# A two-layer decoder trunk: mask set-up, the last block of layer 0, the last gate tile and the last row re-staged

## Chip, cores and metric

The kernel runs on one core of one Trainium2 chip. The metric is the device time of the program in microseconds, the median of three runs. A profiled execution of the same program gives the trace.

## The reference

Input x is 1024 tokens by 1024 channels in float32. Each of two layers adds a mixer of the RMS-normed input to it, and a final RMS norm follows.

```python
# layer 0: gated linear attention (4 heads) beside RWKV-7 (8 heads), chunks of 64 tokens
h = h + (concat(gla, rwkv) * silu(gate)) @ w_out0
# layer 1: q, k, v, gate = rmsnorm(h) @ w_in1 + b; 128-token window, sinks, 16 heads
p = exp(s - m); denom = sum(p) + exp(sink - m)
h = h + ((p / denom) @ v * silu(gate)) @ w_out1 + b_out1
return rmsnorm(h, final_norm_w)
```

RWKV-7 updates a state S = S diag(w) + (S a) b + v k for every token; the kernel solves blocks of it as triangular systems.

## The kernel before, in words

Engines work in program order and meet through semaphores. Three blocks follow each other; all engines leave a block together and enter the next. SyncE (SP) issues all DMAs, in the order in which they are written down.

`project0` norms and turns x, then runs 30 tiles of 128 output columns of layer 0's input projection. Each weight tile arrives by a load, GpSimd (POOL) splits it into a high and a low part (`split_parts`, L1484 and L1488), TensorE (PE) forms three products for each of two halves of 512 tokens (`products3`, L1496), and ScalarE (ACT) keeps the result. VectorE (DVE) works on it; its last operations follow the GLA tiles, n = 14 to 17. The tiles n = 22 to 29 are the gate. At n = 17, 23 and 27 SP spills keys, the GLA's queries and keys (`QK`, the upper half of `VQ`) and values.

`chunks0` is the recurrence, eight blocks of 128 tokens (`ND` = 8), software-pipelined over steps p. Before the steps, SP loads `maska`, `inner`, `maskb`, `maskd` (L702 to L704) and then the first spilled blocks. DVE folds the masks into `near` and `first`, scales `bdones` into `RB`, builds `eye` (L1289 to L1294); ACT fills six buffers from `eye` (L1443, L1444); POOL clears buffers (`zeroed`). PE does `cross(0)` (L848), DVE keeps it under the mask `inner` (`keep_cross`, L1158) and `keep_first_turned` (L1165, L1172), then PE does `near_and_gla(0)` (L860, L865), DVE `keep_products(0)` (L1179, L1182), PE the first join (L877). `RB` is read by `bonus_sums` (L1033). Two steps behind, `output_products` (L1047) multiplies a block by the output weights in two halves of 512 columns; `add_output` (L1276) adds the residual, `square_row` (L1425 to L1430), `invert_row` (L1283) and `norm_row` (L1438) norm the row in place once its un-normed form has been stored to `h1_dram` (L736).

`layer1_stage` turns the normed rows (`turn_rows`, L1708) in 16 groups of four transposes over four banks; ACT keeps the high part of each (L1847), DVE the low part (`low`, L1906). `project_values` (L1496, columns of 256) starts after the tenth group and needs `WVH` and `WVL`, split by POOL (L1484, L1488). Eight value products and 18 tiles follow (8 query, 2 key, 8 gate). In the last tile (n = 17), `scores(0)` and `scores(1)` stand between the halves. Attention is 64 steps g, eight query pairs for each of eight blocks: PE does `scores(g)` (L1735) and `turn_probs(g - 2)` (L1746), DVE `mask_and_max(g)` (L1920) and every other copy of turned probabilities (L1992), ACT two exponentials (L1879) and the other copies (L1873). Every four steps the denominators are inverted (L1934, L1936), turned by PE (`turn_sums`, L1753, first at g = 7), kept (L1941), sent through `es_dram` and spread over the partitions (`spread_sums`), POOL multiplies the gate by them (`scale_gate`, L1679) and DVE gates the values' products (L1946, from g = 13). POOL also stages the next block (`stage`) and splits the output weights (`weights`).

At the end PE forms the output products row by row (L1773, `done`), DVE adds two halves (L2003), ACT squares and roots the row (L1889, L1891), DVE inverts and scales it (`finish`, L1951, L1953), one row behind except for the last, and SP stores it (L1623).

## Time and profile before

| | |
|---|---|
| Median of three runs | 1205.45 us (1202.07 to 1209.12) |
| The profiled execution | 1204.18 us |
| Its span, first to last instruction | 1202.4 us |
| Mean granted TensorE clock | 0.973 |
| PE, DVE, ACT, POOL busy | 1131.1, 532.8, 364.5, 405.7 us |

A row's start is in microseconds from the span's start. The layer 0 tiles end at about 378, the recurrence at about 748, the tiles of layer 1 at about 985, attention at about 1098. A granted clock of 1.00 stands for TensorE's 2.4 GHz, 0.50 for 1.2 GHz. Names of buffers can be those of a buffer that shares the memory.

### The profile page before, as it was taken

The numbers are of one execution on the slowest core, as the hardware profiler recorded it, in microseconds if no ns is written. First come the engines' busy times: TensorE is split into PE (matmuls) and PEld (weight loads), VectorE is DVE, ScalarE is ACT, GpSimd is POOL, SyncE is SP. The second block draws the span as 40 slices with busy tenths as digits, with TensorE's granted clock in tenths as the row PEclk, the third lists the DMA queues.
The fourth block names the chain that finished last, engine by engine and source line by source line (L and its number), as shares of the span: only waits on it lengthen the run. The fifth ranks groups of instructions, "written<-read, shape, count | busy, mean of one in ns | idle before, by whom it ended". The sixth has DMA issues, their size and how long they took to land. (4 is left out here: it accounts for less than half of the span.)

```text
span 1202.4 us, 26513 instructions
## 1 busy us (share of the span) xinstructions
PE 1131.1 (94%) x11544; PEld 855.9 (71%) x11544; DVE 532.8 (44%) x953; ACT 364.5 (30%) x835; POOL 405.7 (34%) x284
## 2 busy tenths in 40 slices
PE   5999999999996899999999997899999989999897
PEld 4777778788885777667666653888888875556785
DVE  5588886510001344344444321525550018995333
ACT  6343432520111233133323322300111027774111
POOL 2223232433331112122212221412333456773752
PEclk9999999999998788999999999899999999999999
DMA  6111102614302311022111113201111112223311
GB/s 252 35 36 52 35 18 71 192 53 122 122 35 96 130 56 43 26 63 73 29 55 46 39 37 104 85 18 53 52 36 51 52 36 62 72 63 92 137 53 70
DMA packets 60024, 82.83 MB, mean 69 GB/s; under 512 B 3200, under 2 KB 45200, under 8 KB 59536
## 3 DMA queue, kind: packets, MB, share of 16 engines
q1 hardware_dynamic: 59920, 81.30, 21.2%
q8 instruction: 82, 1.34, 0.5%
q14 instruction: 22, 0.18, 0.1%
HBM read 64.45 MB, written 16.84 MB: 68 GB/s over the span
## 5 line engine op out<-in xcount | busy, mean ns | idle before, releaser
L1496 PE MATMUL ps<-HNH,WH 128*128 128x512 f32 x736 | 289.9, 394 | 0.0
L1496 PE MATMUL ps<-HNL,WH 128*128 128x512 f32 x736 | 286.4, 389 | 0.0
L1496 PE MATMUL ps<-HNH,WL 128*128 128x512 f32 x736 | 286.4, 389 | 0.0
L1496 PEld LDWEIGHTS ps<-HNH,WH 128*128 128x128 f32 x736 | 138.2, 188 | 31.0 <-issue 2.7
L1496 PEld LDWEIGHTS ps<-HNH,WL 128*128 128x128 f32 x736 | 138.2, 188 | 30.4 <-issue 1.9
L1496 PEld LDWEIGHTS ps<-HNL,WH 128*128 128x128 f32 x736 | 138.2, 188 | 28.9
L1920 DVE CUSTOM_DVE_ANT_0 AR<-ps,GV,nsink 128x256 f32<-128x256 f32 x128 | 56.4, 478 | 89.8 <-PE ps L1735 89.7
L1047 PE MATMUL ps<-VQ,BK 128*128 128x512 f32 x128 | 66.6, 624 | 4.1 <-POOL BK L799 2.2
L1879 ACT ACTIVATE AR<-AR,nm 128x256 f32<-128x256 f32 x128 | 63.6, 499 | 16.6 <-DVE nm L1920 16.6
L1484 POOL CAST WH<-WA 128x1024 fp32r<-128x1024 f32 x16 | 19.1, 1195 | 136.6 <-PE ps L1496 106.9
L1047 PE MATMUL ps<-WO,BK 128*128 128x512 f32 x128 | 64.9, 619 | 0.0
L1484 POOL CAST WH<-GV 128x1024 fp32r<-128x1024 f32 x18 | 18.7, 1041 | 135.7 <-PE ps L1496 135.7
L1285 DVE MEMSET small<- 128x1 f32 x1 | 0.1, 59 | 129.6 <-PEq L232 129.6
L1773 PE MATMUL ps<-HNH,WH 128*128 128x512 f32 x128 | 51.1, 399 | 3.0 <-POOL WL L1647 3.0
L1773 PE MATMUL ps<-HNH,WL 128*128 128x512 f32 x128 | 50.6, 395 | 0.0
L1773 PE MATMUL ps<-HNL,WH 128*128 128x512 f32 x128 | 50.4, 393 | 0.0
L1746 PE MATMUL ps<-ident,AR 128*128 128x128 f32 x256 | 44.2, 298 | 3.1 <-ACT AR L1879 3.1
L877 PEld LDWEIGHTS ps<-shared,GV 64*64 64x64 f32 x1024 | 37.5, 148 | 11.4 <-issue 10.3
L1488 POOL TENSOR_TENSOR WL<-GV,WH 128x1024 fp32r<-128x1024 f32 x18 | 43.2, 2400 | 2.6 <-POOL WH L1484 2.2
L1187 DVE COPY_PREDICATED shared<-near,ps 128x256 f32<-128x256 int32 x32 | 13.8, 433 | 64.5 <-PE ps L877 64.5
L877 PE MATMUL ps<-shared,GV 64*64 64x32 f32 x1024 | 40.1, 230 | 1.5 <-DVE GA L1182 0.9
L1488 POOL TENSOR_TENSOR WL<-WA,WH 128x1024 fp32r<-128x1024 f32 x16 | 39.4, 2460 | 2.1 <-POOL WH L1484 1.4
(288 smaller groups left out, 2000.3 us busy)
## 6 DMA issues: line engine op xcount, KB each, us to landing
GV<-in_w1t SPq DMA_DIRECT2D x18, 512.0 KB, 3.5
AR<-in_x SPq DMA_DIRECT2D x16, 512.0 KB, 5.4
WA<-in_w0t SPq DMA_DIRECT2D x16, 512.0 KB, 3.5
RAW<-in_w0t SPq DMA_DIRECT2D x8, 512.0 KB, 3.8
bk_dram<-BK SPq DMA_DIRECT2D x1, 4096.0 KB, 17.2
RAW<-bk_dram SPq DMA_DIRECT2D x8, 512.0 KB, 5.7
h_dram<-AR SPq DMA_DIRECT2D x8, 512.0 KB, 3.4
GV<-es_dram SPq DMA_DIRECT2D x32, 128.0 KB, 3.0
```

The source lines that it names most:

```text
L877: last = pe.matmul(bank[4][half(e), h * B:(h + 1) * B], BA[d % 2][half(e), a, q, 0, :], x[half(e), h, :], start=True, stop=True)
L1047: last = pe.matmul(bank[5][:], SG[:, k, tokens(d)], WO[k // PAIRS][:, k % PAIRS, h * HB:(h + 1) * HB], start=(k == 0), stop=(k == KT - 1))
L1187: dve.copy_predicated(TM[l][:], near[:, l].unsqueeze(1).to_broadcast([P, HEADS, B]), bank[4][:, 0:HEADS * B].rearrange("p (h t) -> p h t", ...
L1285: dve.memset(leps, LN_EPS)
L1484: eng.tensor_copy(high, raw).then_inc(parts, 1)
L1488: eng.tensor_tensor(low, raw, high.bitcast(F), ALU.subtract).then_inc(parts, 1)
L1496: last = pe.matmul(out, a, b, start=(k == 0 and i == 0), stop=(k == n - 1 and i == 2))
L1746: last = pe.transpose(PS[4 + t % 2][:, (2 * a + b) * P:(2 * a + b + 1) * P], PR[:, t % 3, a, b * P:(b + 1) * P], ident[:])
L1773: last = pe.matmul(PS[2 * (t % 4) + h][:], a[:, (t + 1) % 2, k, :], w[:, k, cols], start=(k == 0 and m == 0), stop=(k == KT - 1 and m == 2 ...
L1879: ins = act.activation(PR[:, g % 3, a, :], PR[:, g % 3, a, :], ACT.Exp, scale=-1.0, bias=nm[:, h:h + 1], accum_out=rs[:, h:h + 1])
L1920: ins = dve.tensor_tensor_reduce(PR[:, g % 3, a, :], PS[2 * (j % 2) + a][:, 0:2 * P], band[:, 0 if n == 0 else 1, :], -1.0, nsink[:, h:h + 1],
```

## The change

Masks. `inner`, `near` (now five levels, as many as are read), `first` and `eye` are allocated for all of layer 0. SP loads three masks in `project0` behind tile 25's weights, into the spilled memory of `QK`; DVE folds them behind its last GLA operations. In `chunks0` only `maska` is loaded; DVE starts with `keep_cross`, and `RB` follows `keep_products(0)`. ACT fills `XT0` first.

```diff
                 if n == 23:
                     sp.wait_ge(g_scaled, 4)
                     spill(1, QK.rearrange("p a q t -> p (a q) t"))
+                if n == 25:
+                    sp.wait_ge(spilled[1], 16)
+                    sp.dma_start(inner[:], maska_d).then_inc(masks_in, 16)
+                    sp.dma_start(maskb, maskb_d[:, 0]).then_inc(masks_in, 16)
+                    sp.dma_start(maskd, maskd_d).then_inc(masks_in, 16)
...
                 dve.tensor_tensor(qk, qk, e, ALU.mult).then_inc(g_scaled, 1)
+            dve.wait_ge(masks_in, 48)
+            for e in range(2):
+                dve.memset(inner[e * C:e * C + B, 0, B:C], 0.0)
+            dve.tensor_tensor(near[:], maskd[:, 0:LEVELS - 1, 0:B], maskd[:, 0:LEVELS - 1, B:C], ALU.bitwise_or)
+            dve.tensor_tensor(first[:], maskb[:, 0, :], maskb[:, 1, :], ALU.bitwise_or)
+            dve.tensor_tensor(eye[:], istack[:, 0:B], istack[:, B:C], ALU.add).then_inc(masks_set, 1)
...
     maska = buf("maska", [P, 2, C])
-    near = buf("near", [P, LEVELS, B], I32)
-    first = buf("first", [P, C], I32)
-    inner = buf("inner", [P, 2, C])
+    inner, near, first, eye = presets
...
-            for mask in (maska, inner):
-                sp.dma_start(mask[:], maska_d).then_inc(s["masks_in"], 16)
-            sp.dma_start(maskb, maskb_d[:, 0]).then_inc(s["masks_in"], 16)
-            sp.dma_start(maskd, maskd_d).then_inc(s["masks_in"], 16)
+            sp.dma_start(maska[:], maska_d).then_inc(s["masks_in"], 16)
...
-                after(pe, "masks_set", 1)
+                after(pe, "masks_set", 2)
...
             dve.memset(leps, LN_EPS)
             dve.memset(geps, EPS)
+            keep_cross(BA, 0, inner, "b_prod", "ba_kept")
+            dve.wait_ge(s["presets"], 1)
+            keep_first_turned(0)
             dve.wait_ge(s["masks_in"], 64)
-            for e in range(2):
-                dve.memset(inner[QTR[2 * e][2], 0, B:C], 0.0)
-            dve.tensor_tensor(near[:], maskd[:, :, 0:B], maskd[:, :, B:C], ALU.bitwise_or)
-            dve.tensor_tensor(first[:], maskb[:, 0, :], maskb[:, 1, :], ALU.bitwise_or)
+            dve.wait_ge(s["zeroed"], 1)
+            keep_products(0)
             for q in range(PAIRS):
-                dve.tensor_scalar(RB[:, q, :], bdones[:], col("r_k", q), None, ALU.mult)
-            dve.tensor_tensor(eye, istack[:, 0:B], istack[:, B:C], ALU.add).then_inc(s["masks_set"], 1)
-            dve.wait_ge(s["masks_set"], 1)
-            dve.wait_ge(s["presets"], 1)
-            dve.wait_ge(s["zeroed"], 1)
-            keep_cross(BA, 0, inner, "b_prod", "ba_kept")
-            keep_first_turned(0)
-            keep_products(0)
+                ins = dve.tensor_scalar(RB[:, q, :], bdones[:], col("r_k", q), None, ALU.mult)
+            ins.then_inc(s["masks_set"], 1)
...
-            act.wait_ge(s["masks_set"], 1)
-            for b in TM:
-                act.activation(b[:], eye.unsqueeze(1).to_broadcast([P, HEADS, B]), ACT.Copy)
-            act.activation(XT0[:], eye.unsqueeze(1).to_broadcast([P, HEADS, B]), ACT.Copy).then_inc(s["presets"], 1)
+            for b in (XT0, *TM):
+                ins = act.activation(b[:], eye[:].unsqueeze(1).to_broadcast([P, HEADS, B]), ACT.Copy)
+            ins.then_inc(s["presets"], 1)
```

The last block. The second half of the last output product is added, squared and normed in layer 1's block. POOL writes the normed row to a part of `VQ`, between the two halves of the `WV` split, and the transposes read it there; the store, too, is issued in the new block. The value products start two groups later. ACT waits for the stores before it overwrites the rows.

```diff
             def add_output(d, h):
-                if not 0 <= d < ND:
+                if not 0 <= d < ND or (d, h) == (ND - 1, 1):
                     return
...
-                if not 0 <= d < ND:
+                if not 0 <= d < ND - 1:
...
             def square_row(d):
                 if not 0 <= d < ND:
                     return
+                if d == ND - 1:
+                    after(act, "out_added", 2 * d + 1)
+                    act.wait_ge(s["gated"], d + 1)
+                    act.activation(VT[:, :, tokens(d)], H1[:, 0:PAIRS, tokens(d)], ACT.Square, accum_out=ms[:, d:d + 1]
+                                   ).then_inc(s["half"], 1)
+                    act.wait_ge(s["half"], 3 * d + 1)
+                    act.activation(mb[:, d:d + 1], ms[:, d:d + 1], ACT.Identity, bias=eps, scale=1.0 / D).then_inc(s["half"], 1)
+                    return
...
+            sp.wait_ge(s["out_added"], 2 * TT)
+            sp.dma_start(h1_dram[:, TT - 1, :].rearrange("p (k c) -> p k c", c=P), AR[:, :, last_block]
+                         ).then_inc(h1_out[(TT - 1) % 2], 16)
+            for dst, src in ((BV, bv1), (COS, cos_d), (SIN, sin_d)):
+                sp.dma_start(dst, src).then_inc(s["rope_in"], 16)
             for there in h1_out:
                 sp.wait_ge(there, 16 * TT // 2)
-            for dst, src in ((BV, bv1), (COS, cos_d), (SIN, sin_d)):
-                sp.dma_start(dst, src).then_inc(s["rope_in"], 16)
...
             pool.wait_ge(wv_in, 16)
-            split_parts(pool, WV, WVH, WVL, 2 * W0_TILES, parts)
+            pool.tensor_copy(WVH, WV).then_inc(parts, 1)
+            pool.wait_ge(s["inverted"], 2 * TT)
+            pool.tensor_scalar(last_row, AR[:, :, last_block], last_rs, None, ALU.mult).then_inc(s["normed"], 1)
+            pool.wait_ge(parts, 2 * W0_TILES + 1)
+            pool.tensor_tensor(WVL, WV, WVH.bitcast(F), ALU.subtract).then_inc(parts, 1)
...
+                if g == KT:
+                    pe.wait_ge(s["normed"], TT)
                 for j in range(4):
-                    last = pe.transpose(PS[g % 4][:, j * P:(j + 1) * P], AR[:, k, block_tokens(4 * half + j)], ident[:])
+                    t = 4 * half + j
+                    last = pe.transpose(PS[g % 4][:, j * P:(j + 1) * P], last_row[:, k, :] if t == TT - 1 else
+                                        AR[:, k, block_tokens(t)], ident[:])
...
             for g in range(KT):
                 turn_rows(g)
             for g in range(KT, 2 * KT):
                 turn_rows(g)
-                if g % 2:
-                    project_values((g - KT) // 2)
-            for t in range(TT // 2, TT):
+                if g % 2 and g > KT + 1:
+                    project_values((g - KT) // 2 - 1)
+            for t in range(TT // 2 - 1, TT):
                 project_values(t)
...
+            act.wait_ge(s["out_added"], 2 * TT)
+            act.activation(VQ[:, 0:KT // 2, last_block], AR[:, KT // 2:, last_block], ACT.Square, accum_out=last_ms
+                           ).then_inc(s["half"], 1)
+            act.wait_ge(s["half"], 3 * TT)
+            act.activation(last_ms, last_ms, ACT.Sqrt, bias=last_mb, scale=1.0 / D).then_inc(s["rooted"], 1)
...
+            for there in h1_out:
+                act.wait_ge(there, 16 * TT // 2)
...
+            added = AR[:, KT // 2:, last_block]
+            dve.tensor_tensor(added, added, PS[5][:].rearrange("p (k t) -> p k t", k=KT // 2), ALU.add
+                              ).then_inc(s["out_added"], 1)
             dve.memset(KTT[:, :, 0:P], 0.0)
             dve.memset(V1[:, 0, :], 0.0)
+            dve.wait_ge(s["rooted"], 2 * TT)
+            dve.reciprocal(last_rs, last_ms).then_inc(s["inverted"], 1)
+            for g in range(KT):
+                low(g)
             dve.tensor_scalar(bqs, col("b_q", 0, 8), GLA_SCALE, None, ALU.mult).then_inc(s["bq"], 1)
             dve.tensor_scalar(nsink[:], col("sinks", 0, 16), -1.0, None, ALU.mult).then_inc(s["bq"], 1)
             dve.wait_ge(s["bq"], 2)
-            for g in range(KT):
-                low(g)
             dve.wait_ge(s["rope_in"], 48)
             for g in range(KT, 2 * KT):
                 low(g)
-                if g % 2:
-                    keep_values((g - KT) // 2)
-            for t in range(TT // 2, TT):
+                if g % 2 and g > KT + 1:
+                    keep_values((g - KT) // 2 - 1)
+            for t in range(TT // 2 - 1, TT):
```

The last gate tile. Its first half has SiLU while PE works on the second. Its second half is kept as exp(-x) and as x, POOL adds 1, DVE inverts it in step 4, and POOL multiplies by x between the first two splits of output weights.

```diff
                 sp.wait_ge(s["sums_out"], 16 * (half + 1))
                 if half:
                     sp.wait_ge(s["scaled"], half)
+                else:
+                    sp.wait_ge(s["chain"], 4 * (Q_TILES + 2) + 3)
...
-            pool.wait_ge(s["tile_done"], W1_TILES)
+            pool.wait_ge(s["tile_kept"], W1_TILES + 2)
+            gate = SG1[:, KT - 1, HB:]
+            pool.tensor_scalar(gate, gate, 1.0, None, ALU.add).then_inc(s["chain"], 1)
             def scale_gate(half):
                 pool.wait_ge(s["sums_in"], 32 * (half + 1))
+                if half == HALVES // 2 + 1:
+                    pool.wait_ge(s["chain"], 4 * (Q_TILES + 2) + 3)
                 pool.tensor_tensor(place(half), place(half), RD, ALU.mult).then_inc(s["scaled"], 1)
 
             weights(0)
+            pool.wait_ge(s["chain"], 4 * (Q_TILES + 2) + 2)
+            pool.tensor_tensor(gate, LAST, gate, ALU.mult).then_inc(s["chain"], 1)
...
-                tile_half(n % 2, 0)
+                first = tile_half(n % 2, 0)
                 if n == W1_TILES - 1:
+                    first.then_inc(s["tile_done"], 1)
                     scores(0)
                     scores(1)
                 tile_half(n % 2, 1).then_inc(s["tile_done"], 1)
...
                 if g == 2:
-                    pe.wait_ge(s["tile_kept"], W1_TILES)
+                    pe.wait_ge(s["tile_kept"], W1_TILES - 1)
+                if g == 6:
+                    pe.wait_ge(s["tile_kept"], W1_TILES + 2)
                 if g - 2 < STEPS:
...
-            for j in range(KT):
+            for j in range(KT - 1):
                 keep(W1_GATE + j, SG1[:, j, :], ACT.Silu)
+            act.wait_ge(s["tile_done"], W1_TILES)
+            act.activation(SG1[:, KT - 1, 0:HB], PS[6][:], ACT.Silu).then_inc(s["tile_kept"], 1)
 
             for g in range(STEPS + 2):
                 t = g - 2
+                if t == 0:
+                    act.wait_ge(s["tile_done"], W1_TILES + 1)
+                    act.activation(SG1[:, KT - 1, HB:], PS[7][:], ACT.Exp, scale=-1.0).then_inc(s["tile_kept"], 1)
+                    act.activation(LAST, PS[7][:], ACT.Copy).then_inc(s["tile_kept"], 1)
...
+                if g == 4:
+                    dve.wait_ge(s["chain"], 4 * (Q_TILES + 2) + 1)
+                    dve.reciprocal(SG1[:, KT - 1, HB:], SG1[:, KT - 1, HB:]).then_inc(s["chain"], 1)
```

The last row. PE signals each half; each half is added and squared by itself. POOL multiplies the first half by the final norm's weights; at the end ACT scales the first half while DVE scales the second.

```diff
-                sp.wait_ge(s["normed"], TT + t + 1)
+                sp.wait_ge(s["normed"], TT + t + (2 if t == TT - 1 else 1))
...
+            pool.wait_ge(s["squared"], 2 * TT)
+            pool.tensor_tensor(R[:, TT - 1, 0:HB], R[:, TT - 1, 0:HB], FN[:, 0:HB], ALU.mult).then_inc(s["biased"], 1)
...
-                if i == 2 * KT - 1:
+                if i == 2 * KT - 1 or (t, i) == (TT - 1, KT - 1):
                     last.then_inc(s["done"], 1)
...
+            t = TT - 1
+            act.wait_ge(s["added"], TT)
+            act.activation(SW[:, 0:HB], R[:, t, 0:HB], ACT.Square, accum_out=ms[:, t:t + 1]).then_inc(s["squared"], 1)
+            act.wait_ge(s["squared"], 2 * TT)
+            act.activation(first_half, ms[:, t:t + 1], ACT.Identity, bias=eps, scale=1.0 / D).then_inc(s["squared"], 1)
+            act.wait_ge(s["added"], TT + 1)
+            act.wait_ge(s["squared"], 2 * TT + 1)
+            act.activation(SW[:, HB:T], R[:, t, HB:T], ACT.Square, accum_out=ms[:, t:t + 1]).then_inc(s["squared"], 1)
+            act.wait_ge(s["squared"], 2 * TT + 2)
+            act.activation(sd[:, t:t + 1], ms[:, t:t + 1], ACT.Sqrt, bias=first_half, scale=1.0 / D).then_inc(s["rooted"], 1)
+            act.wait_ge(s["biased"], TT + 1)
+            act.wait_ge(s["inverted"], 3 * TT)
+            act.activation(R[:, t, 0:HB], R[:, t, 0:HB], ACT.Copy, scale=sd[:, t:t + 1]).then_inc(s["normed"], 1)
...
+                cols = slice(HB if t == TT - 1 else 0, T)
+                dve.scalar_tensor_tensor(out=R[:, t, cols], in0=R[:, t, cols], scalar=sd[:, t:t + 1], in1=FN[:, cols],
                                          op0=ALU.mult, op1=ALU.mult).then_inc(s["normed"], 1)
...
                 for h in range(2):
                     cols = slice(h * HB, (h + 1) * HB)
+                    if t == TT - 1 and h:
+                        finish(t - 1)
+                        dve.wait_ge(s["done"], TT + 1)
                     ins = dve.tensor_tensor(R[:, t, cols], R[:, t, cols], PS[2 * (t % 4) + h][:], ALU.add)
-                ins.then_inc(s["added"], 1)
-                if t:
+                    if t == TT - 1 or h:
+                        ins.then_inc(s["added"], 1)
+                if 0 < t < TT - 1:
                     finish(t - 1)
             finish(TT - 1)
```

## Rows read from the trace of the kernel before

**Rows 1.** The page's first part: busy us (share of the span) and instructions of each engine.

```profile
PE 1131.1 (94%) x11544; PEld 855.9 (71%) x11544; DVE 532.8 (44%) x953; ACT 364.5 (30%) x835; POOL 405.7 (34%) x284
```

**Rows 2.** TensorE's waits: line, releaser, us in total, times, longest.

```profile
PE ps L860 <- DVE shared L1165: 10.6, 1, 10.6
...
PE ps L1708 <- PEq L698: 5.5, 1, 5.5
...
PE ps L1746 <- ACT AR L1879: 3.1, 1, 3.1
PE ps L1773 <- POOL WL L1647: 3.0, 1, 3.0
```

**Rows 3.** Timeline of VectorE at the start of the recurrence: start, us, operation, idle before.

```profile
379.81 0.06 DVE L1285 MEMSET small<- 128x1 f32 x1 [129.64 <-PEq L232]
...
388.64 1.23 DVE L1158 TENSOR_TENSOR GV<-ps,inner 128x1024 f32<-128x1024 f32 x1 [2.07 <-issue]
```

**Rows 4.** Timeline of TensorE at the start of the recurrence.

```profile
379.78 1.10 PE L848 MATMUL ps<-AR,RAW 64*64 64x128 f32 x32 [1.43 <-PEq L232]
391.50 0.88 PE L860 MATMUL ps<-RAW,AR 64*32 64x32 f32 x64 [10.62 <-DVE shared L1165]
```

**Rows 5.** Timeline of ScalarE at the start of the recurrence.

```profile
386.61 1.64 ACT L1443 ACTIVATE shared<-OB 128x256 f32<-128x256 f32 x5 [7.13 <-DVE OB L1294]
```

**Rows 6.** Timeline of SyncE at the start of the recurrence.

```profile
381.83 0.36 SPq L710 DMA_DIRECT2D QKS<-qk_dram  x1
```

**Rows 7.** DMA issues: size and median us to landing.

```profile
out<-AR SPq DMA_DIRECT2D x8, 512.0 KB, 2.6
...
QKS<-qk_dram SPq DMA_DIRECT2D x8, 256.0 KB, 3.1
```

**Rows 8.** Timeline of all engines at the entry of layer 1.

```profile
748.87 0.63 ACT L1425 ACTIVATE VQ<-AR 128x512 f32<-128x512 f32 x1 [11.46 <-DVE AR L1276]
...
752.14 1.15 ACT L1438 ACTIVATE AR<-AR,small 128x1024 f32<-128x1024 f32 x1 [1.14 <-DMA h_dram<-AR]
...
753.60 6.76 PE L1708 MATMUL ps<-ident,AR 128*128 128x128 f32 x36 [5.48 <-PEq L698]
...
755.54 4.55 POOL L1488 TENSOR_TENSOR KHL<-GV,Q 128x2048 fp32r<-128x2048 f32 x1
...
755.60 7.50 DVE L1906 SCALAR_TENSOR_TENSOR HNL<-ps,par,HNH 128x512 fp32r<-128x512 f32 x10
...
761.92 0.36 PE L1496 MATMUL ps<-Q,HNH 128*128 128x256 f32 x1 [0.75 <-DVE HNL L1906]
```

**Rows 9.** Groups of instructions on GpSimd by form: busy us, mean ns.

```profile
L1652 POOL TENSOR_TENSOR AR<-AR,KTT 128x1024 f32<-128x1024 f32 x8 | 24.0, 3006 | 0.0
```

**Rows 10.** Timeline of ScalarE behind the last gate tile.

```profile
984.84 1.08 ACT L1853 ACTIVATE VQ<-ps 128x512 f32<-128x512 f32 x2 [10.96 <-PE ps L1496]
985.95 1.28 ACT L1879 ACT_TABLE_LOAD   x1
```

**Rows 11.** Groups of instructions on VectorE by form.

```profile
L1920 DVE CUSTOM_DVE_ANT_0 AR<-ps,GV,nsink 128x256 f32<-128x256 f32 x128 | 56.4, 478 | 89.8 <-PE ps L1735 89.7
L573 DVE RECIPROCAL GV<-GV 128x1024 f32<-128x1024 f32 x4 | 26.2, 6552 | 0.1
```

**Rows 12.** Chain of waits around the first turned denominators.

```profile
997.51 0.21 PE ps L1753
```

**Rows 13.** Busy time by stretch: PE, PEld, DVE, ACT, POOL, granted clock, DMA.

```profile
988.00:998.00 10.00, 9.52 (x48) 6.91 (x49) 6.01 (x22) 7.20 (x28) 3.68 (x3) 0.50 0.36 106
...
1116.00:1121.00 5.00, 5.00 (x15) 3.94 (x16) 1.28 (x2) 1.46 (x3) 5.00 (x3) 0.66 1.00 404
```

**Rows 14.** Timeline of VectorE and SyncE behind the last matmul.

```profile
1194.09 1.28 DVE L2003 TENSOR_TENSOR AR<-AR,ps 128x512 f32<-128x512 f32 x2 [8.20 <-PE ps L1773]
...
1196.79 1.97 SPq L1623 DMA_DIRECT2D out<-AR  x2
...
1197.11 1.28 DVE L1953 SCALAR_TENSOR_TENSOR AR<-AR,small,V 128x1024 f32<-128x1024 f32 x1
```

More of the change, by code:

```diff
@@ L103, in trunk @@
         rms = {n: sem("rms_" + n) for n in ("squared", "rooted", "inverted")}
-        rows = {n: sem("rows_" + n) for n in ("done", "added", "normed")}
+        rows = {n: sem("rows_" + n) for n in ("done", "added", "normed", "out_added", "half")}
         def row_turn():
@@ L145, in trunk @@
             bk_in0 = sem("bk_in0")
+            inner = sb("inner", [P, 2, C], ctx=layer0)
+            near = sb("near", [P, LEVELS - 1, C // 2], I32, ctx=layer0)
+            eye = sb("eye", [P, C // 2], ctx=layer0)
+            first = sb("first", [P, C], I32, ctx=layer0)
+            presets = (inner, near, first, eye)
+            preset_sems = {n: sem("c_" + n) for n in ("masks_in", "masks_set")}
             half1 = ExitStack()
@@ L630, in chunks0 @@
     maska = buf("maska", [P, 2, C])
-    near = buf("near", [P, LEVELS, B], I32)
-    first = buf("first", [P, C], I32)
-    inner = buf("inner", [P, 2, C])
+    inner, near, first, eye = presets
     BK = key_blocks
@@ L1885, in _ @@
                         act.activation(es[:, hs], es[:, hs], ACT.Exp).then_inc(s["es_exp"], 1)
-            for t in range(TT):
+            for t in range(TT - 1):
                 act.wait_ge(s["added"], t + 1)
```

41 lines of the change are left out of this document (25 added, 16 removed).

## The prediction

> **What bounds the kernel now.** The page comes first: TensorE is busy for 94% of the span [rows 1], so nearly every microsecond not spent in its instructions is one it waited for. The waits of PE are read next: four of them are named by this change [rows 2], 10.6 us at the start of the recurrence (L860), 5.5 at the entry of layer 1 (L1708), 3.1 at the first probabilities (L1746), and the 3.0 at L1773 that the change leaves alone. The timelines then tell which wait ends last at each place, and the last one shows the tail behind the last matmul. All times below are against the profiled execution, 1204.18 us (span 1202.4); the median of the three runs is 1205.45, 1.27 above it. About 0.5%, 6 us, is what a measurement can tell from no change.
>
> **Part A, masks.** Before, VectorE enters the recurrence at 379.81 and its first product with `inner` starts only at 388.64 [rows 3]: in between lie four mask loads, the folds, `RB`, `eye`, and ScalarE's six fills. PE has finished `cross` at 379.78 + 1.10 = 380.88 and starts `near_and_gla` at 391.50 [rows 4]. After, inner, maskb and maskd are loaded and folded among layer 0's gate tiles, where VectorE idles for 129.6 us [rows 3]; the three load issues and their wait stand on SyncE's queue before the load of tile 26, behind a spill that was issued two tiles earlier, so I cost them at nothing (cover: a whole tile; without it, at most the three issues, about 1.3 us). Then the product starts at 380.9. From it to `near_and_gla` the kernel before took 391.50 - 388.64 = 2.86 us, all VectorE work that stays: 383.8. Three other things must be there. The fills take 0.33 each [rows 5], six from 379.8, `XT0` among them: 381.8, before the 382.2 at which they are needed. `maska` is the first load, needed at 385. The load of QK is issued at 381.83 behind four mask loads [rows 6]; now it stands behind one, about 380.1, with 0.36 of issue and 3.1 to landing [rows 7]: 383.6, just in time. **Gain 391.5 - 383.8 = 7.7 us.** `RB`'s four multiplications (0.86 in all) now stand behind `keep_products`, beside PE's first join (1.9 us), and the bonus sums that wait for them come several microseconds later: nothing. Bounds: 5 us, if the QK load lands as late as 386.5; 9, if the clock is kept too.
>
> **Part B, last block.** Before, PE ends at about 748.1 (5.48 before 753.60); then come the add, ScalarE's two squares from 748.87, root, reciprocal, the wait for the row's store, a scaling of 1.15 at 752.14, the barrier, and PE starts at 753.60 [rows 8]. After, the block ends with PE: transposes from about 748.5. The new critical chain is on VectorE and ScalarE: add 0.69 (749.15), one half square with its read-out 0.75, root 0.3, reciprocal 0.2 (750.4), and only then `high(0)` 0.69 and eight `low` passes, at 0.75 each (ten in 7.5 us [rows 8]): 750.95 + 6.0 = 756.95. Beside it, on POOL: the 1.9 us cast of `WVH`, the new `last_row` multiplication, and `WVL`'s 4.55 [rows 8], which `last_row` now stands ahead of. For `last_row` no row exists (POOL has no tensor_scalar here). Bounds: half of `WVH`'s cast (0.95) and the 3.0 us bias addition of the same 128x1024 [rows 9]; I take 2.4, POOL's usual two-operand pass of that size, since the output is not a plain cast. So `parts` is complete at 748.45 + 1.9 + 2.4 + 4.6 = 757.4. The first value product was at 761.92 [rows 8] and is now at 757.5, with two more groups of transposes (0.87 us) already behind it: **gain 4.4 + 0.9 = 5.3 us**, bounds 4.4 to 5.5. The bq and nsink operations (1.5 us) stand behind `low(7)` now and are covered by that first value product (2.9 us). The row's store and the three table loads on SyncE come in the new block within 2 us, and are first needed behind the first value product; the splits of W1 slip by 2.4 us relative to it, with eight value groups of 2.9 us as cover.
>
> **Part C, first exponentials.** Before, PE waits 3.1 us, to 988.5, for SiLU (1.08) and the table load (1.28) that stand before the first exponential [rows 2, 10]. After, half 0's SiLU, the load and steps 0 and 1 lie under half 1, and PE runs on. But the second half of the gate becomes exp, a copy, POOL's + 1, and a **VectorE reciprocal**. That operation costs 6.55 us on 128x1024 [rows 11], so 3.28 on 128x512, and stands in step 4. By the step order: masks (two passes of 0.48 [rows 11], about 0.85 a step) and copies put it at 989.65 to 992.95; step 5's mask, and then the denominators, end at 994.2. PE, which has got to `turn_sums(0)` at 990.7, waits 3.5 us there. Before, it did `turn_sums(0)` at 997.51 [rows 12], after six steps at half clock. So even with the new wait PE is there 3.2 us earlier. But a wait of that length did not pass without the clock here: after the 3.1 us one the granted clock was 0.50 for all of 988 to 998, though PE was busy 9.5 of the 10 us; after the 3.0 us one at L1773 the stretch 1116:1121 shows 0.66 [rows 13]. If the new wait does the same, the steps from 994 on run at 1.2 GHz for a time that was at full clock before. Price: half of 9.5 us (4.7) by the nearest row, the same instructions; half of 3.4 by the other. I take 4.7: **loss 4.7 - 3.2 = 1.5 us**; bounds a gain of 3.2 and a loss of 3. POOL's + 1 and its multiplication (about 1.3 each) delay `weights(1)`; `stage(2)` still starts at about 998, as before, with ten steps in hand. SyncE's first `spread_sums` waits behind both; its result is first needed at step 13.
>
> "TensorE: Matmul & The Clock Gate" of the Trainium skill, section "HAM oscillation", says that a kernel whose matmul bursts are separated by waits pays the slow clock anew after each. By it the sum is the one above; without it part C would be a gain of 3.2. By that rule, the trace agrees [rows 13].
>
> **Part D, last row.** Before: adds from 1194.09 (two, 1.28), square, root, reciprocal, scaling from 1197.11 for 1.28, end at 1202.4 [rows 14]. After, the first half is added, squared and multiplied by FN (POOL) under the last 5.4 us of matmuls; row 6 is finished there too. Behind them: add 0.65, square 0.8, root 0.3, reciprocal 0.2, two halves side by side on VectorE and ScalarE 0.65: 1.3 to 1.5 us less. And the last two stores no longer overlap: before they were issued 1.6 us apart, and the last landed about 3.4 after its issue against a median of 2.6 [rows 7, 14]: 0.7. **Gain 2.2**, bounds 1.3 to 2.6.
>
> **Sum:** 7.7 + 5.3 - 1.5 + 2.2 = 13.7; 1204.18 - 13.7 = **1190.5 us**. The profiled execution is a little below the median; I leave that difference in the range.
>
> **The rivals.**
> 1. *The clock holds in part C.* PE is busy for five microseconds around the new wait, and the drop came here at different lengths of idleness. Then C is a gain of 3.2, and the time 1204.18 - 18.4 = 1185.8. Against: both waits of 3 us were followed by half clock [rows 2, 13].
> 2. *A transfer or the clock takes part of A and B.* The QK load lands late (A 5.2), or the transposes at layer 1's entry, now spaced by 0.75 us low passes with PE busy for about half of that, leave PE at half clock in the first value products, 3 us. Either gives 1193 to 1194, both 1196.
> 3. *The POOL multiplication is slow* and the change ends slower than before. Place: `last_row`, before `WVL`, with PE's second half of transposes waiting for it. Its price adds one for one beyond 2.4 us. It decides from 2.4 + 13.7 = 16 us for 1024 columns; at 25 us the time is 1213. Against: no POOL operation of this size takes more than 3.0 us in the mean here.
> 4. *The change doesn't do what it says*: A's masks are folded early, but another wait, the fills or `zeroed`, holds the start: A 3 us, 1195. Against: POOL's memsets end at 381.8.
>
> **How the numbers follow.** Forecast 0.45, rival 1 0.25, rival 2 0.20, rival 3 0.02, rival 4 0.08. Range: from the clock holding (1185.8) with a microsecond or two of better luck in A, to rival 2 with both parts and the 1.27 of the median: 1184 to 1197. Slower by over 0.5% only in rival 3 (0.02). Within 0.5% needs gains below 6 us: small tails of rivals 2 and 4, 0.06. Faster: 0.92.
>
> **What would show it.** In the profile after: `near_and_gla` about 3 us behind `cross`; no long PE wait at the first transposes of layer 1, the first value product about 9 us behind the last output product; a reciprocal of about 3.3 us on VectorE in step 4 and a PE wait of 3 to 4 us at `turn_sums`, with the clock at 0.50 behind it; the last store alone. It would be wrong if the L860 wait stays above 5 us, if `last_row` takes over 4, or if the attention section is longer than before by over 3.

## The result, and the profile after

The changed kernel took 1195.32 us (median of 20 runs, 1186.36 to 1206.16), the kernel before, beside it, 1206.64 (20 runs): a ratio of 0.9905, 95% interval 0.9884 to 0.9925, 11.4 us less. The profiled execution took 1191.37, its span 1189.6 against 1202.4, so the pair of traces differs by 12.8 us. A ratio leaves out executions in the slow state (over 1.5% above the fastest of the same kernel), so it is not always the quotient of the medians given beside it. Both kernels scatter by 14 to 20 us, and with the clock: one run of the changed kernel had a mean granted clock of 0.986 and a span of 1184.6 us, another 0.966 and 1204.4.

The page's first part [rows 1], then TensorE's waits [rows 2]: line, releaser, us in total, times, longest.

```profile
PE 1129.1 (95%) x11544; PEld 852.2 (72%) x11544; DVE 539.8 (45%) x954; ACT 365.1 (31%) x839; POOL 412.7 (35%) x288
```

```profile
PE ps L1799 <- DVE es L2011: 7.3, 6, 3.7
...
PE ps L878 <- DVE shared L1183: 2.9, 1, 2.9
PE ps L1819 <- POOL WL L1677: 2.8, 1, 2.8
...
PE ps L1753 <- DVE HNL L1981: 1.3, 1, 1.3
PE ps L1516 <- POOL KHL L1689: 1.1, 1, 1.1
...
PE ps L1792 <- ACT AR L1941: 0.6, 2, 0.4
```

The 10.6 us at the start of the recurrence became 2.9, the 5.5 at layer 1's entry became 1.3 and 1.1, the 3.1 at the first probabilities 0.6 (two waits). New is the 3.7 at the first turned sums (L1799).

**A.** Timelines of the start of the recurrence: start, us, engine, operation, idle before [rows 3, 4, 5, 6].

```profile
381.78 1.10 PE L866 MATMUL ps<-AR,RAW 64*64 64x128 f32 x32 [1.43 <-PEq L246]
385.81 0.82 PE L878 MATMUL ps<-RAW,AR 64*32 64x32 f32 x64 [2.93 <-DVE shared L1183]
...
382.94 1.23 DVE L1176 TENSOR_TENSOR GV<-ps,inner 128x1024 f32<-128x1024 f32 x1 [0.68 <-PE ps L866]
...
381.76 1.95 ACT L1463 ACTIVATE shared<-eye 128x256 f32<-128x256 f32 x6 [0.28 <-PEq L246]
...
382.17 0.37 SPq L728 DMA_DIRECT2D QKS<-qk_dram  x1
```

From the first product of `cross` to the first of `near_and_gla`: 385.81 - 381.78 = 4.03 us, before 391.50 - 379.78 = 11.72. A is worth 7.69.

**B.** The entry of layer 1 [rows 8].

```profile
744.01 1.94 PE L1753 MATMUL ps<-ident,AR 128*128 128x128 f32 x16 [0.32 <-PEq L719]
747.20 3.18 PE L1753 MATMUL ps<-ident,AR 128*128 128x128 f32 x19 [1.25 <-DVE HNL L1981]
...
753.51 0.39 PE L1516 MATMUL ps<-Q,HNH 128*128 128x256 f32 x1 [1.05 <-POOL KHL L1689]
...
746.39 5.36 DVE L1981 SCALAR_TENSOR_TENSOR HNL<-ps,par,HNH 128x512 fp32r<-128x512 f32 x8 [0.41 <-ACT HNH L1896]
...
743.98 1.89 POOL L1685 CAST Q<-GV 128x2048 fp32r<-128x2048 f32 x1 [15.46 <-POOLq L719]
746.09 2.85 POOL L1687 TENSOR_SCALAR VQ<-AR,small 128x1024 f32<-128x1024 f32 x1 [0.21 <-DVE small L2038]
748.91 4.55 POOL L1689 TENSOR_TENSOR KHL<-GV,Q 128x2048 fp32r<-128x2048 f32 x1
```

TensorE ends the recurrence at 743.69. The first value product comes 9.82 us behind that, before (761.92, behind 748.12) 13.81, and two more groups of transposes are already done.

**C.** Behind the last gate tile, which ends at 975.57: VectorE, then stretches of all engines (busy us of PE, PEld, DVE, ACT, POOL, granted clock, DMA share, GB/s) [rows 12, 13].

```profile
980.63 3.33 DVE L2076 RECIPROCAL VQ<-VQ 128x512 f32<-128x512 f32 x1
...
985.36 0.20 DVE L2011 RECIPROCAL es<-es 128x8 f32<-128x8 f32 x1
```

```profile
976.00:984.00 8.00, 5.36 (x48) 3.76 (x44) 7.80 (x17) 4.92 (x17) 4.86 (x3) 0.96 0.16 39
984.00:990.00 6.00, 4.38 (x17) 1.99 (x19) 4.88 (x17) 3.86 (x14) 5.88 (x5) 0.50 0.16 46
990.00:1000.00 10.00, 10.00 (x75) 5.71 (x75) 8.24 (x30) 6.47 (x23) 7.56 (x6) 0.99 0.23 75
```

The first turned sums start 10.05 us behind the tile's end (985.62), before 12.50 (997.30), though TensorE waits 3.7 us there. The clock is at 0.50 until 990.

**D.** Behind the last product, which ends at 1183.72 [rows 14].

```profile
1183.76 0.69 DVE L2090 TENSOR_TENSOR AR<-AR,ps 128x512 f32<-128x512 f32 x1 [3.29 <-PE ps L1819]
...
1185.76 0.75 DVE L2029 SCALAR_TENSOR_TENSOR AR<-AR,small,V 128x512 f32<-128x512 f32 x1
```

The pair by stages, us: ahead of the recurrence +2.00 (381.78 against 379.78). That is the clock and not A's masks: the changed kernel's trace has 3.4 us at half clock there, and three traces with A and none there (the two with copies moved and the one with transposes in the recurrence, below) reach `cross` at 379.78 to 379.84, as the kernel before does. Then A -7.69; rest of the recurrence +1.27; last output product to first value product -3.99; from there to the end of the gate tiles 222.06 against 222.88, -0.82; to the first turned sums -2.45; from those to the last product 198.10 against 196.68, +1.42; the tail 5.87 against 8.42, -2.55. Sum -12.8.

### The profile page after: what moved, and what is told of

It reads as the page before. It is cut to its first block and busy times, and to the rows that moved or that the text cites. A ratio compares the mean times of both kernels' runs of the same rounds, so it can differ in the third digit from the quotient of the medians.

```text
span 1189.6 us, 26524 instructions
## 1 busy us (share of the span) xinstructions
PE 1129.1 (95%) x11544; PEld 852.2 (72%) x11544; DVE 539.8 (45%) x954; ACT 365.1 (31%) x839; POOL 412.7 (35%) x288
## 5 line engine op out<-in xcount | busy, mean ns | idle before, releaser
L1902 ACT ACTIVATE AR<-ps,small 128x512 f32<-128x512 f32 x16 | 10.1, 686 | 94.6 <-PE ps L1516 94.6
```

## The experiments

Before each result stands what was expected. "Base" is the kernel before, run beside them on the same chip. The intervals are at 95%.

### Each part alone

Each kernel is the one before with one part's edits from the diff above and none of the others; a line of each tells which.

```diff
+    inner, near, first, eye = presets
```

> Part A alone on the kernel before (masks loaded and folded in layer 0's gate tiles, cross product first, RB behind the first products). Theory 1, every part saves what its stage shows: from the end of cross(0) to near_and_gla(0) 2.9 us instead of 10.6, and the program 7.7 us shorter (ratio 0.9936). Theory 2, the clock takes part of it back: the same 7.7 us in that stage, but the recurrence behind it longer at half clock by 2 to 4 us, so that the program is 4 to 6 us shorter (0.995 to 0.997).

```diff
+            pool.tensor_scalar(last_row, AR[:, :, last_block], last_rs, None, ALU.mult).then_inc(s["normed"], 1)
```

> Part B alone (the last block finished in layer 1's block). Theory 1: from the last output product to the first value product 9.8 us instead of 13.8, with two transposes groups more behind it, 4.9 us in all (ratio 0.996); POOL's WVL, not VectorE's low passes, ends the wait. Theory 2: the transposes, spaced by the low passes, leave PE at half clock in the first value products in some executions: 2 to 4 us (0.997 to 0.998).

```diff
+                    dve.reciprocal(SG1[:, KT - 1, HB:], SG1[:, KT - 1, HB:]).then_inc(s["chain"], 1)
```

> Part C alone (the last gate tile's second half by exp, + 1, reciprocal). Theory 1: the 3.1 us wait of PE goes, a wait of 3.5 to 3.7 us at the first turned denominators comes, with half clock for 5 to 10 us behind it: between a gain of 1.5 and a loss of 1.5 us (0.999 to 1.001). Theory 2, the reciprocal is covered elsewhere: the whole 3.1 us is gained (0.9974).

```diff
+                cols = slice(HB if t == TT - 1 else 0, T)
```

> Part D alone (the last row in halves). Theory 1: from the last matmul to the end 5.9 us instead of 8.4, 2.5 us shorter (0.998). Rival: the last store's landing takes back what its earlier issue gives, 1.3 us (0.999).

Measured against base at 1207.21 us (35 runs), 12 runs each: A 0.9923 (0.9896 to 0.9950); B 0.9931 (0.9904 to 0.9958); C 1.0012 (0.9979 to 1.0046); D 1.0011 (0.9985 to 1.0037). By these ratios A and B carry the change: 9.3 and 8.3 us. C and D can't be told from nothing in totals, and their traces have to say what they do. The start of the recurrence in A alone:

```profile
381.62 1.10 PE L866 MATMUL ps<-AR,RAW 64*64 64x128 f32 x32 [1.43 <-PEq L246]
385.65 0.88 PE L878 MATMUL ps<-RAW,AR 64*32 64x32 f32 x64 [2.92 <-DVE shared L1183]
```

4.03 us again. In B alone the entry takes 9.81 us, and stays at full clock. The clock column (last but two) of that entry, in the kernel before and then in B alone:

```profile
750.00:765.00 15.00, 10.49 (x66) 10.08 (x67) 9.12 (x15) 8.52 (x15) 11.19 (x6) 0.77 0.46 132
```

```profile
740.00:765.00 25.00, 21.51 (x123) 14.78 (x122) 14.62 (x22) 10.71 (x20) 15.89 (x7) 1.00 0.40 127
```

Without the 5.5 us of idle TensorE the slow stretch that followed it (0.77 over 15 us is 6.9 at half clock) is gone, in all ten traces with B; the four without it have 3.4 to 6.8 us there. The slow stretch lay on the transposes: 36 took 6.76 us [rows 8], 0.19 each, with B 16 took 1.94, 0.12 each.

In D alone the last scaling ends 2.82 us behind the last product, in the kernel before, A, B and C alone 4.42: 1.60 gained. From there to the end the last store took 3.99 us in D alone and 4.00 before, 3.05 in A, B and C alone and in the changed kernel. That step of 0.95 us goes with the execution and not with D.

C alone behind its gate tile: the wait of 3.67 us, and the clock at 0.53 over the seven microseconds around it.

```profile
999.87 0.37 PE L1762 MATMUL ps<-ident,es 128*8 128x128 f32 x1 [3.67 <-DVE es L1954]
```

```profile
997.00:1004.00 7.00, 4.13 (x15) 1.81 (x15) 6.12 (x18) 3.86 (x14) 5.64 (x5) 0.53 0.25 75
```

### Everything but C

The changed kernel with the last gate tile in its old order, run twice, the second time beside the changed kernel itself.

```diff
-            for j in range(KT - 1):
+            for j in range(KT):
                 keep(W1_GATE + j, SG1[:, j, :], ACT.Silu)
...
-                    act.activation(SG1[:, KT - 1, HB:], PS[7][:], ACT.Exp, scale=-1.0).then_inc(s["tile_kept"], 1)
-                    act.activation(LAST, PS[7][:], ACT.Copy).then_inc(s["tile_kept"], 1)
...
-                    dve.reciprocal(SG1[:, KT - 1, HB:], SG1[:, KT - 1, HB:]).then_inc(s["chain"], 1)
```

> The changed kernel with part C undone: the last gate tile in its old order, A, B and D kept. Theory 1 (C pays back what it gains: the sums' transpose comes 2.45 us sooner behind the tile's end, and some 4 us of the half-clock time that used to lie beside waiting now lie beside work, worth 2 us): totals as the changed kernel's, ratio to the kernel before 0.990 to 0.993, and in the trace 12.5 us from the tile's end to the first transpose of the sums against 10.05, with at most 1 us of half clock behind that transpose. Rival a (C is a gain, the clock is luck): 2.5 us slower than the changed kernel, 0.9925. Rival b (C is a loss, as the sum of the prediction had it by 1.5 us): 0.989.

> The version without part C once more, in the same call as the changed kernel. Theory 1: ratio 0.988 to 0.992, first sum of exponentials at 9.7 to 10.7 us behind the tile's end (by how much half clock falls ahead of it), the last at 113.5 to 116.5. Rival a: 0.986 to 0.988. Rival b: 0.993.

> The changed kernel once more, on the same chip and beside the same runs of the kernel before as the version without part C, so that the two can be set against each other. Theory 1 (VectorE paces the attention stage, so C neither gains nor costs): ratio 0.988 to 0.992, within 0.3% of the version without C, and the last sum of exponentials 113.5 to 116.5 us behind the end of the last gate tile in both. Rival a (C costs the half clock and the reciprocal in the wait): the changed kernel stays 0.2 to 0.3% above the version without C. Rival b (C is a gain of 2.5 us and the last comparison was luck of the clock): 0.2% below it.

Without C: 1188.11 us, 0.9877 (0.9849 to 0.9905, 6 runs), and again 1193.80, 0.9894 (0.9851 to 0.9936, 7 runs). With C, in the second call: 1197.47, 0.9919 (0.9882 to 0.9956, 12 runs). In both pairs the version without C is faster, by 0.0028 (against the changed kernel's 0.9905 from another call) and 0.0025, about 3 us; the intervals overlap. C alone pointed the same way, 0.0012 above one. So C is no gain in any of three comparisons of totals, and none of them alone proves a loss.

The traces say more. First, what C had to beat is not 12.5 us any more: without it but with B, the sums start 10.17 us behind the tile in every trace (in B alone 11.61; before, and in A and D alone, 12.50). The stretch behind ScalarE's 3.1 us wait is slow for less time: 0.57 over 4 us, where rows 13 show 0.50 for 10.

```profile
976.00:980.00 4.00, 4.00 (x24) 2.84 (x22) 3.72 (x12) 3.25 (x12) 1.94 (x1) 0.57 0.56 159
980.00:990.00 10.00, 10.00 (x76) 5.71 (x74) 8.63 (x38) 8.44 (x30) 6.27 (x5) 1.00 0.18 63
```

So beside B the whole gain of C at this point is 10.17 - 10.05 = 0.12 us. Why B, 222 us earlier, shortens that stretch, no run tells. Second, C has its own slow stretch, partly behind the wait: 6.8 us at half clock, in every trace with C in which the wait stands empty (five). Without C and beside A, B and D it is 3.4, in three traces, and all of it ahead of the first sums. The changed kernel's first three turned sums, and those of the version without C:

```profile
985.62 0.38 PE L1799 MATMUL ps<-ident,es 128*8 128x128 f32 x1 [3.67 <-DVE es L2011]
994.33 0.27 PE L1799 MATMUL ps<-ident,es 128*8 128x128 f32 x1
1001.26 0.27 PE L1799 MATMUL ps<-ident,es 128*8 128x128 f32 x1
```

```profile
981.15 0.27 PE L1790 MATMUL ps<-ident,es 128*8 128x128 f32 x1
987.83 0.27 PE L1790 MATMUL ps<-ident,es 128*8 128x128 f32 x1
994.52 0.27 PE L1790 MATMUL ps<-ident,es 128*8 128x128 f32 x1
```

From the first to the second it is 8.71 us with C and 6.68 without, with no wait in either. The 4.6 us at half clock that C has behind its first sums cost about 2 (8.65 to 9.02 in the five traces, 6.68 or 6.69 in the three). Behind the tile's end the third sums come at 25.7 us with C and at 23.5 without (25.5 to 25.7 in the other traces of the same code). So in this stage C is a loss of 2.1 us beside B. Against the kernel before, whose third sums come at 26.1, it is a gain of 0.5, in C alone of 0.7.

### What the wait at the first sums is made of

The changed kernel without the reciprocal of the last gate half (that half of the gate isn't inverted).

```diff
-                    dve.reciprocal(SG1[:, KT - 1, HB:], SG1[:, KT - 1, HB:]).then_inc(s["chain"], 1)
+                    dve.memset(small[:, 56:57], 0.0).then_inc(s["chain"], 1)
```

> The changed kernel without the reciprocal of the last gate half on VectorE (a write of one column stands in its place, so that half of the gate isn't inverted). It prices what the wait at the first transpose of the sums is made of. Theory 1 (the 3.33 us reciprocal alone holds it, and the half clock follows from the idle TensorE): the wait of 3.7 us falls below 1 us, no half clock behind it, so 3 us of wait and 2 us of clock are gone: ratio 0.986. Rival a (another operation, GpSimd's product or the sum of the exponentials, ends the wait next): the wait falls by 1 us or less and the time stays near 0.990. Rival b (the half clock does not hang on this wait): wait gone, clock still 0.50 behind the transpose, 0.988.

Measured: 1192.47 us, 0.9870 (0.9836 to 0.9905, 12 runs). The wait is gone, and the first sums start 6.48 us behind the tile, with the clock at 1.00 (the stretch 990:1000; the sums are at 990.9). So without the reciprocal there is no such wait. The clock still falls, 10 us later: 3.4 us at half clock from 1000.8, behind a wait of 1.43 us at the second sums (999.5). And most of the 3.57 us gained at the first sums is given back in the trace: the last reciprocal of the sums started 113.6 us behind the tile's end, in the changed kernel 114.8, since TensorE waited for later sums instead (in the changed kernel the same line sums to 7.3, the 3.67 of the first among them):

```profile
PE ps L1799 <- DVE es L2011: 6.5, 7, 1.4
```

6.5 against 3.6. This is one execution of each; the same waits are 2.5 us before and 4.8 in D alone, which are the same code there. The median of the twelve runs is lower than the changed kernel's by more (0.9870 for 0.9905, which is near theory 1's 0.986), but the intervals overlap, and these runs spent less time at half clock (a median of 52 us for 57).

The second half of that question is the clock. Idle transposes keep TensorE at work in the wait:

```diff
                 if g % HT == HT - 1 and 0 <= g - 7 < STEPS:
+                    if g == 7:
+                        for _ in range(24):
+                            pe.transpose(PS[6][:, 0:P], ident[:], ident[:])
                     turn_sums((g - 7) // HT)
```

> The changed kernel with 24 idle transposes of the identity on TensorE ahead of the first transpose of the sums, in the 3.7 us of wait (2.6 us of work at full clock). Nothing else changes. Theory 1 (the idle of TensorE in that wait brings the half clock behind it): the wait stays in sum, the granted clock is 1.00 for the 8 us behind the transpose, and the stretch from there to the last product is 2.3 us shorter (some 195.8 us where its other waits are as in the changed kernel): ratio 0.9885. Rival a (the clock falls by what comes ahead of the wait, the thinner products of the scores): clock still 0.50 there, 0.9905. Rival b (the added transposes end after the sum of exponentials is ready): up to 1 us slower, 0.991.

Measured: 1198.67 us, 0.9943 (0.9914 to 0.9972, 12 runs). The clock held, as theory 1 had it; the time did not fall. The stretches, and the first three turned sums:

```profile
984.00:990.00 6.00, 4.97 (x44) 4.18 (x44) 6.00 (x12) 2.61 (x11) 3.60 (x3) 1.00 0.32 89
990.00:1000.00 10.00, 8.80 (x64) 4.93 (x64) 9.47 (x32) 7.28 (x28) 8.80 (x7) 1.00 0.25 70
```

```profile
990.62 0.27 PE L1799 MATMUL ps<-ident,es 128*8 128x128 f32 x1 [1.05 <-DVE es L2014]
998.05 0.27 PE L1799 MATMUL ps<-ident,es 128*8 128x128 f32 x1 [0.57 <-DVE es L2014]
1006.42 0.27 PE L1799 MATMUL ps<-ident,es 128*8 128x128 f32 x1 [1.52 <-DVE es L2014]
```

The changed kernel has no wait at its second and third sums; here there are two, 2.1 us. The second sums come 7.42 us behind the first (changed kernel 8.71), the third 15.80 (15.64), and the first at the same time behind the tile in both. So the idleness of that wait does bring the half clock; taking it away earned 1.3 us up to the second sums and nothing up to the third. The third sums' wait ended with an operation of VectorE that takes 0.16 us elsewhere; here it ran until GpSimd's beside it had ended:

```profile
1004.04 2.09 DVE L2012 TENSOR_TENSOR es<-es,rs_ 128x8 f32<-128x8 f32 x1
```

```profile
1003.75 2.36 POOL L1508 TENSOR_TENSOR HNL<-SW,HNH 128x1024 fp32r<-128x1024 f32 x1
```

The stage as a whole can't tell: 198.95 us from the first sums to the last product, in the changed kernel 198.10 and 201.41. Why the total is 3 us above the changed kernel's no stage of this trace tells; the intervals overlap a little.

### Does VectorE pace the attention stage?

The waits for the sums end on VectorE, which was busy 65.65 of 70 us in that stage. I took it for the pace, and moved a quarter of the copies to ScalarE, 16 of 64 (the expectation has 8 by an error), with C and without it. The counts that TensorE waits for follow.

```diff
     def on_dve(t):
-        return t % 2 == 0
+        return t % 4 == 0
...
```

> The changed kernel with a quarter of the copies of the turned probabilities moved from VectorE to ScalarE (8 of 0.68 us leave VectorE, 8 of some 0.55 us go to ScalarE). Theory 1 (VectorE, 14 of every 14 to 15 us busy there, paces the attention stage and gives back what C gained): the last sum of exponentials comes at 109 to 112 us behind the tile's end instead of 114.8, TensorE's waits for the sums behind the first fall from 3.6 us to under 1.5, the stage is 2 to 4 us shorter: ratio 0.987 to 0.9885. Rival a (the waits come from the chain's own latency, ScalarE's exponentials among it): ScalarE's added copies delay the exponentials, waits as before or longer, 0.990 to 0.993. Rival b (VectorE's time is not its copies but its short operations held while GpSimd works): under 1 us gained.

> The same move of copies from VectorE to ScalarE in the version without part C. Theory 1 (VectorE paced the stage in both): 2 to 4 us below the version without C, ratio 0.985 to 0.988; and with VectorE relieved, C should count for something: its 2.5 us at the first transpose of the sums, less its half clock, so this one is 0 to 1.5 us slower or as fast as the changed kernel with the same move. Rival a (C is a loss in any case): 2 us or more faster than that one.

Measured: with C 1195.43 us, 0.9927 (0.9892 to 0.9963, 9 runs); without C 1191.07, 0.9875 (0.9834 to 0.9916, 11 runs). 70 us of the attention stage (PE, PEld, DVE, ACT, POOL), first in the changed kernel run again, then with the copies moved:

```profile
1001.00:1071.00 70.00, 67.40 (x490) 37.91 (x486) 65.65 (x228) 52.24 (x188) 55.15 (x40) 1.00 0.24 69
```

```profile
990.00:1060.00 70.00, 67.59 (x492) 38.04 (x490) 59.27 (x217) 56.27 (x198) 54.59 (x41) 1.00 0.24 70
```

VectorE lost 6.4 us of work, TensorE's share didn't move, the waits for the sums behind the first were 3.0 us against 3.3, and the last reciprocal of the sums started 113.8 us behind the tile's end, not 109 to 112. VectorE's copies do not pace the stage; my theory fell, though the ratio without C lies in its range: it would lie there without the move as well (0.9877). TensorE is busy 96 to 97% of the stage. The waits that are left are those of rival b, VectorE's short operations held while GpSimd works. In all fourteen traces TensorE waits 76 times over 0.15 us at a turned sum behind the first, 53.5 us in all. Ahead of each stands a VectorE sum of denominators (`es<-es,rs_`, 128x8) that took 0.68 us or more instead of 0.16 and ended 0.02 to 0.03 us behind a two-input operation of GpSimd. So the first edit to try is in GpSimd's order; no run here has it. These waits scatter from 2.5 to 6.5 us between executions, so a part of C's size can't be read from the whole stage of a pair of traces. The pair with the copies moved is a third one in which the version without C is faster (0.0052).

### The half clock in the recurrence

```diff
             cross(0, BK[0][:, 0], "b_prod", swapped)
+            for _ in range(24):
+                pe.transpose(bank[6][:, 0:P], ident[:], ident[:])
             near_and_gla(0)
```

> The changed kernel with 24 idle transposes of the identity between the first cross products of the recurrence and the first near products, in the 2.9 us of wait that part A left there. Theory 1 (that idle, and the 1.4 us before it, bring the half clock of 386 to 413): clock 1.00 from 386 on, half-clock time of the execution down from 47 us by some 20 us, worth 7 to 10 us: ratio 0.982 to 0.985. Rival a (the recurrence's first block brings the clock down by itself, its products being small and its DMA and VectorE chain long; the spell only begins later): 0.989 to 0.991. Rival b (the added transposes delay the near products): 0.5 us slower.

Measured: 1196.09 us, 0.9917 (0.9886 to 0.9947, 6 runs): rival a. The transposes fill the wait (2.84 us of work, then 0.15 idle), and the clock falls all the same:

```profile
384.00:388.00 4.00, 2.47 (x140) 0.91 1.03 330
388.00:396.00 8.00, 7.83 (x164) 0.50 0.96 408
396.00:410.00 14.00, 13.05 (x309) 0.50 0.19 62
410.00:432.00 22.00, 19.71 (x452) 0.59 0.06 16
```

The columns are the stretch, TensorE busy, granted clock, DMA share, GB/s. The clock fell at 387.25. Ahead of that TensorE had waited 0.99 us at the first join (from 384.94), once the added transposes were done; behind it, it was busy 7.83 of 8 us at half clock. Filling the wait that A left does not keep the clock up here, though the same 24 transposes did so in the attention stage. Whether the wait at the join brings the fall is untested.

## Why the prediction was right, point by point

**The total.** 13.7 us were predicted against the profiled 1204.18, 12.8 came in the pair of traces, and 11.4 by the ratio. That 12.8 is so near is in part luck: 0.95 of it is the last store's, 3.3 us are lost ahead of the recurrence and in the rest of it, and C was wrong in both of its terms. A and B make nearly all of it, as forecast.

**A: right, 7.7 predicted, 7.69 measured** (4.03 against 11.72, in all ten traces that hold A). The fills ended at 383.71, the QK load was issued 0.39 us behind `cross`'s start, and neither held the start. The load of the masks ahead, put at nothing, costs nothing (`cross` at 379.8 with and without it, where no slow clock stands ahead). Rivals 2 and 4 did not occur here. A alone gave 9.3 us in totals (6.0 to 12.6), more than the trace's step but not surely so.

**B: right in mechanism, 5.3 predicted, 4.8 in the stages** (3.99 + 0.82). The mis-sized term is `last_row` on GpSimd: taken at 2.4, it took 2.85 and began 0.21 us behind the cast, so `WVL` ended last and the first value product came at 9.8 instead of 9.4 us. (The other branch has a slip: 750.4 and `high(0)`'s 0.69 are 751.1, not 750.95; it ended before `WVL` all the same, 8.1 us behind the last output product.) The two groups of transposes done early were put at 0.87 and show as 0.82 less behind the first value product. Rival 2 looked for half clock at this place as a danger of B; the kernel before had it, and B removed it. In totals B alone was worth 8.3 (5.1 to 11.6): 0.9 us more are in the trace at the first sums (11.61 for 12.50), and beside A and D 2.3; the prediction had neither.

**C: a loss of 1.5 predicted; both terms of the sum were too large.** The new wait is as foreseen: a reciprocal of 3.33 us (3.28), a wait of 3.67 (3.5), half clock behind it. The term most mis-sized is the price of that half clock, half of 9.5 us or 4.7: the slow stretch is 6.8 us long, 4.6 of it behind the sums' start, and they cost about 2 us up to the second sums (8.71 for 6.68). The kernel with the clock kept got only 1.3 of them and lost those by the third sums, to VectorE's operations held by GpSimd. The 3.2 gained at the first sums was 2.45: rows 12 give 997.51, a piece of the chain, where the operation starts at 997.30, and VectorE's sum took 0.72 us beside GpSimd's new product instead of 0.16. So in the prediction's own terms C gives 2.45 - 2.0, a gain of 0.4 against the kernel before, not a loss. Beside B it is a loss of 2.1, but for a reason that the prediction doesn't have: B had taken the gain already (0.12 us of it are left). Where the totals point to a loss, the sign is right by luck.

"HAM oscillation" in "TensorE: Matmul & The Clock Gate" of the Trainium skill says that matmul bursts separated by waits pay the slow clock anew, and it counts half of the slow time as lost. The trace agrees for this wait (0.50 with it, 1.00 with it filled), and nearly with the half (2.0 of 4.6 us).

**D: 2.2 predicted, 1.6 measured.** The computing part was put at 1.3 to 1.5 and is 1.60. The 0.7 for a store that no longer overlaps another is not borne out: the last store took 3.99 us in one execution of D's form and 3.05 in nine others, 4.00 in one of the old form and 3.05 in three.

**Sum by measured steps:** A 7.7, B 4.8 up to the end of the gate tiles, B and C together 0.5 from there to the third turned sums, D 1.6: 14.6.

**The range.** Most of what is left is the clock in the recurrence. From `near_and_gla` to the last output product the 13 traces and the one before take 353.5 to 364.4 us, and the longest are those with the most time at half clock. A line fitted to all runs of this study, with a level for each kernel, gives 0.38 us of span for each us at half clock (twice the span times one less the mean clock), and leaves 1.6 us unexplained in a run. With 60 us of half clock for all it puts base at 1202 and the changed kernel 7.5 below. Against the base runs of their own call A alone is 5.3 below, B 3.4, D 0.5, and C 1.3 above, each with a standard error near 0.5; the version without C is 1.4 below the changed kernel. The line takes every us at half clock for equally dear, and it isn't: in the traces of kernels without A, 7 to 8 us of it lie in the very wait that A removes, where they cost nothing, and that would account for A's 5.3 instead of 7.7. Of the ratio's 11.4 the rest, some 4 us, goes in part with less time at half clock: the median is 57 us in the changed kernel's twenty runs, 55 in A alone, 51 in B alone and 65 in the base runs beside these two. At 0.38 us each that is 3; one is left without a cause.

## What to carry to other kernels

Price a stall of TensorE by the work behind it as well: here removing a 5.5 us idle also removed 6.9 us at half clock. Half the length of a slow stretch is a fair price only for the part behind the wait (2.0 us for 4.6 here; the prediction took 9.5 us of slow clock), and avoiding it pays only if the next wait doesn't take it back. When two edits shorten neighbouring waits, cost the second against the kernel that has the first: C's 2.45 us were 0.12 beside B. And before you put a wait down to a busy engine, look at the duration of the one operation that ends it, against its own shortest.

The version without C was the fastest measured (0.9877 and 0.9894; with copies moved to ScalarE 0.9875), though its intervals overlap with the changed kernel's.

## What was not expected of the hardware

An identical VectorE operation takes 0.16 or 1.56 us (0.14 to 2.09 over all traces), by what GpSimd does. In the version without C, VectorE's 128x8 sum started at 1044.20 while GpSimd's operation ran to 1045.74, and ended with it at 1045.76; the next one, with GpSimd idle, took 0.16. The copies and the fused operations beside them kept their times.

```profile
1044.20 1.56 DVE L1991 TENSOR_TENSOR es<-es,rs_ 128x8 f32<-128x8 f32 x1
...
1052.04 0.16 DVE L1991 TENSOR_TENSOR es<-es,rs_ 128x8 f32<-128x8 f32 x1
```

```profile
1043.37 2.37 POOL L1661 TENSOR_TENSOR Q<-AR,Q 128x1024 fp32r<-128x1024 f32 x1
```

"SBUF — State Buffer" of the Trainium skill says it in "SBUF: two separate sides": a VectorE operation with two inputs in SBUF and a GpSimd operation share a port pair, and whichever is second waits for the whole of the other. The trace agrees, to 0.02 us. The 32 small sums on `es` take 14.2 us before and 16 to 22 in the other traces, so some of VectorE's busy time is waiting. This is what ends TensorE's waits at the turned sums, and why taking copies off VectorE did not shorten them.

In the recurrence's first block the clock stays down with TensorE busy 7.83 of 8 us; in the changed kernel it rose 27 us after its fall, in the kernel with the transposes 24, without a change in that share that I could name. What brings it down and up there stays open.
